# One-time chunk slots ahead of a weight ring, 32x32 block turns on the vector engine, and two w_down rows a partition in a one-core MoE encoder layer

## What is computed

```python
logits = xf @ w_router + b_router           # 32 experts
top_val, top_idx = lax.top_k(logits, 4)
gates = softmax(top_val)
# for each expert e, over the tokens that chose it:
hu = xb @ w_gate_up[e] + b_gate_up[e]       # 1024 -> 2 * 1024
a = minimum(hu[:, :1024], 7)
lin = clip(hu[:, 1024:], -7, 7)
act = a * sigmoid(1.702 * a) * (lin + 1)
y[tok] += (act @ w_down[e] + b_down[e]) * g
# then a last norm over x + y
```

## Time and profile before

| | us |
|---|---|
| median of 3 runs | 1447.47 |
| the profiled execution | 1449.7 |
| its span, from the first to the last instruction | 1447.7 |
| TensorE busy | 1354.7 |
| VectorE busy | 495.0 |
| ScalarE busy | 241.2 |
| GpSimd busy | 380.3 |

### The profile page before, as it was taken

How to read it: one execution, slowest core, us unless ns; L and a number is a source line. 1 busy time by engine, 2 the same in 40 slices (tenths; PEclk the granted TensorE clock), 3 DMA queues, 4 the chain that set the end, 5 groups by cost and what they waited for, 6 DMA issues and landing times.

```text
span 1447.7 us, 34000 instructions
## 1 busy us (share of the span) xinstructions
PE 1354.7 (94%) x14238; PEld 669.4 (46%) x14238; DVE 495.0 (34%) x791; ACT 241.2 (17%) x378; POOL 380.3 (26%) x298
## 2 busy tenths in 40 slices
PE   4899999987999999999999999999999999999982
PEld 4876777862444444444444433333344434344431
DVE  5555553552222223332322222222233333223222
ACT  4333333220111111111111111111111111111112
POOL 6834237034122211211122222111122111111110
PEclk9999999989999999999999999999999999999996
DMA  7511112565999999999999999999999999999994
GB/s 210 129 33 55 59 59 93 223 253 213 364 388 381 385 380 374 381 373 378 390 382 371 377 393 378 371 383 371 373 380 382 379 379 383 371 378 393 391 376 131
DMA packets 112780, 451.12 MB, mean 312 GB/s; under 512 B 14065, under 2 KB 38657, under 8 KB 79952
## 3 DMA queue, kind: packets, MB, share of 16 engines
q1 hardware_dynamic: 99664, 426.27, 77.1%
q0 software_dynamic: 10768, 19.86, 6.0%
q10 hardware_dynamic: 2320, 4.59, 0.8%
HBM read 440.01 MB, written 19.25 MB: 317 GB/s over the span
## 4 chain that ended last, share of the span: by engine, by line
DMA 62%; PE 27%; DVE 5%; issue 3%; ACT 2%; POOL 1%; SPq 1%; DVEq 0%; ACTq 0%; POOLq 0%
DMA raw<-in_w_gate_up_dram 16%; DMA raw_b<-in_w_down_dram 16%; DMA raw_a<-in_w_down_dram 15%; DMA raw_c<-in_w_gate_up_dram 14%; PE bank L1423 8%; PE bank L1439 4%; PE bank L1199 4%; PE bank L1201 4%; PE bank L1200 4%; DVE probs L977 1%; PE bank L1289 1%; ACT probs L720 1%; PE bank L1253 1%; DVE probs L964 1%; PE bank L1387 1%
## 5 line engine op out<-in xcount | busy, mean ns | idle before, releaser
L1423 PE MATMUL bank<-raw,xT 128*32 128x512 f32 x2304 | 343.7, 594 | 8.6 <-issue 4.1
L1425 PE MATMUL bank<-raw,xT 128*32 128x512 f32 x768 | 339.3, 594 | 0.2
L1125 DVE TENSOR_TENSOR gate_in<-bank,b_bc 96x512 f32<-96x512 f32 x64 | 41.1, 682 | 643.9 <-PE bank L1425 643.9
L1423 PEld LDWEIGHTS bank<-raw,xT 128*32 128x32 f32 x2304 | 90.6, 110 | 230.3 <-issue 189.5
L1439 PE MATMUL bank<-raw_a,aT 128*32 128x256 f32 x2232 | 166.8, 380 | 0.0
L1442 PE MATMUL bank<-raw_a,aT 128*32 128x256 f32 x744 | 166.4, 380 | 0.0
L1423 PE MATMUL bank<-raw_c,xT 128*32 128x512 f32 x1116 | 165.5, 592 | 0.0
L1425 PE MATMUL bank<-raw_c,xT 128*32 128x512 f32 x372 | 164.7, 592 | 0.0
L577 POOL DMA_INDIRECT sum_rows<-y_out,scatter_list x32 | 47.4, 1482 | 443.2 <-ACT y_out L831 364.6
L1439 PEld LDWEIGHTS bank<-raw_a,aT 128*32 128x32 f32 x2232 | 88.8, 110 | 62.1
L1439 PE MATMUL bank<-raw_b,aT 128*32 128x256 f32 x1152 | 93.1, 393 | 13.8 <-DMA raw_b<-in_w_down_dram 10.2
(11 more groups left out here) (227 smaller groups left out, 2259.1 us busy)
## 6 DMA issues: line engine op xcount, KB each, us to landing
raw<-in_w_gate_up_dram SPq DMA_DIRECT2D x128, 1024.0 KB
raw_c<-in_w_gate_up_dram SPq DMA_DIRECT2D x62, 1024.0 KB, 7.7
raw_a<-in_w_down_dram SPq DMA_DIRECT2D x62, 1024.0 KB
raw_b<-in_w_gate_up_dram SPq DMA_DIRECT2D x32, 1024.0 KB, 5.6
raw_b<-in_w_down_dram SPq DMA_DIRECT2D x32, 1024.0 KB, 9.1
raw_e<-in_w_gate_up_dram SPq DMA_DIRECT2D x31, 1024.0 KB
raw_d<-in_w_down_dram SPq DMA_DIRECT2D x31, 1024.0 KB
raw<-in_w_in_dram SPq DMA_DIRECT2D x24, 512.0 KB, 5.3
```

The source lines that it names most:

```text
L1125: dve.tensor_tensor(gate_in[0:TILE, cols], bank[n][0:TILE, :], b_bc[0:TILE, cols], ALU.add)
L1423: pe.matmul(bank[r][c * GROUP:(c + 1) * GROUP, :], xT[:, i, c * GROUP:(c + 1) * GROUP], w[:, r * 512:(r + 1) * 512], start=first, stop=last)
L1425: ins = pe.matmul(bank[r][TILE:P, :], xT[:, i, r * GROUP:(r + 1) * GROUP], w[:, 1536:2048], start=first, stop=last)
```

## The change

Four things. (1) Chunks 0 to 5 go to six slots of their own, used once; from chunk 6 on there is a ring of 12, so there are 18 slots, in memory that lay unused behind the front (`raw_f`, `raw_g`). Chunk m from 18 on still waits for chunk m - 12 to be used. (2) TensorE's 16 transposes a job and ScalarE's four copies are gone: VectorE turns `x_got` into `xT` (`turn_x`) and `lin_in` into `aT` (`turn_act`) by 12 transposes of 32x32 blocks each, straight in SBUF. (3) A down chunk puts rows 2p and 2p + 1 of `w_down` in partition p, one run of 8 KB in place of two of 4 KB; `turn_act` reads the activations with a stride of two to match. (4) The order of the jobs' parts: on VectorE `take_gu(j)`, `turn_x(j + 1)`, `clamp(j)`, `gate(j)`, `take_y(j - 1)`, `turn_act(j)`; GpSimd scatters job j - 1 (before: j - 2) in job j, loads the scatter list before it spreads the down biases, and spreads the gate-up biases ahead of the scatter; the loops start at job 2 on all engines but TensorE, where it starts at job 1.

```diff
-RAW = 12
+AHEAD, RING = 6, 12
+RAW = AHEAD + RING
...
-            for ring in (raw01, raw_a, raw_d, raw_b, raw_e, raw_c):
-                if m < ring.shape[1]:
-                    return ring[:, m, :]
-                m -= ring.shape[1]
+        def slot_of(m):
+            return m if m < AHEAD else AHEAD + (m - AHEAD) % RING
+        def raw_slot(slot):
+            for ring in (raw01, raw_a, raw_f, raw_d, raw_b, raw_g, raw_e, raw_c):
+                if slot < ring.shape[1]:
+                    return ring[:, slot, :]
+                slot -= ring.shape[1]
+        def loads(m, b):
+            return 16 if m < AHEAD else later(16 * ((m - AHEAD) // RING + 1), b, 16)
...
-                sp.dma_start(raw_slot(m % RAW).rearrange("p (i n) -> p i n", i=2),
-                             w_down[0, e, 2 * i * P:2 * (i + 1) * P, :].rearrange("(i p) n -> p i n", p=P))\
-                  .then_inc(w_loaded[m % RAW], 16)
...
+                sp.dma_start(raw_slot(slot_of(m)).rearrange("p (i n) -> p i n", i=2),
+                             w_down[0, e, 2 * i * P:2 * (i + 1) * P, :].rearrange("(p i) n -> p i n", i=2))\
+                  .then_inc(w_loaded[slot_of(m)], 16)
+            def wait_slot(m, b):
+                used = fixed(sp, later(m - (RING - 1), b, JOB)) if m >= RAW else 0
                 if m >= RAW:
                     sp.wait_ge(w_used, used)
                     return
...
                 elif m == RAW_FRONT + 2:
+                    sp.wait_ge(mT_hi_ready, KD)
+                    sp.wait_ge(mT_lo_ready, KD)
+                elif m == RAW_FRONT + 4:
                     sp.wait_ge(lists_emptied, 16)
-                elif m == RAW_FRONT + 3:
+                elif m == RAW_FRONT + 5:
                     wait_used(sp, N_FRONT - 1)
-                elif m == RAW_FRONT + 5:
+                elif m == RAW_FRONT + 11:
                     sp.wait_ge(ss_1_ready, TT)
-                elif m == RAW_FRONT + 6:
+                elif m == RAW_FRONT + 12:
                     sp.wait_ge(router_ready, TT)
...
                 gather(j + 1)
-                if n > 1:
-                    dn_loads = scatter(j - 2, lambda: fixed(pool, j * 16))
-                else:
-                    dn_loads = j * 16
-                gu_loads = fixed(pool, j * 16 + 16)
+                gu_loads = fixed(pool, j * 16 + 32)
+                pool.wait_ge(b_gu_loaded, gu_loads)
+                dn_loads = fixed(pool, j * 16 + 16)
+                spread_gu()
+                row = scatter(j - 1, lambda: list_row(j))
                 pool.wait_ge(b_dn_loaded, dn_loads)
-                pool.wait_ge(b_gu_loaded, gu_loads)
-                row = list_row(j - 1)
+                load_scatter_list(j, row)
                 spread_dn()
-                spread_gu()
-                load_scatter_list(j - 1, row)
+            pool.wait_ge(b_dn_loaded, 16)
+            spread_dn()
+            load_scatter_list(0, list_row(0))
+            pool.wait_ge(b_gu_loaded, 32)
+            spread_gu()
             job(1)
-            count = bodies(pool)
+            count = jobs_after(pool, 2)
             with pool.Fori(0, count) as b:
...
+                job(2, b)
...
-                load_bias_gu(j)
-                if n > 1:
-                    scale_y(j - 2)
-                    load_bias_dn(j - 1)
-                turned(j - 1, aT, act_turned, aT_ready)
-                turned(j + 1, xT, got_turned, xT_ready)
+                load_bias_gu(j + 1)
                 sigmoid(j)
-            turned(1, xT, got_turned, xT_ready)
+                scale_y(j - 1)
+                load_bias_dn(j)
+            take_picks()
+            load_bias_gu(1)
+            sigmoid(0)
             job(1)
...
+            def take_gu(j, used):
...
                 ins.then_inc(gu_taken, 1)
+            def turn_x(j):
+                dve.wait_ge(x_gathered, j * 16)
+                for g in range(GROUPS):
+                    rows = x_got[g * GROUP:(g + 1) * GROUP, :].rearrange("t (k q p) -> t k q p", q=QUADS, p=GROUP)
+                    for q in range(QUADS):
+                        ins = dve.transpose(xT[q * GROUP:(q + 1) * GROUP, :, g * GROUP:(g + 1) * GROUP], rows[:, :, q, :])
+                ins.then_inc(got_turned, 1)
...
+            def turn_act(j, used):
+                dve.wait_ge(act_ready, j + 1)
+                if not (isinstance(j, int) and j == 0):
+                    dve.wait_ge(w_used, used)
+                for g in range(GROUPS):
+                    rows = lin_in[g * GROUP:(g + 1) * GROUP, :].rearrange("t (i q p h) -> t i h q p", q=QUADS, p=GROUP, h=2)
+                    for q in range(QUADS):
+                        ins = dve.transpose(aT[q * GROUP:(q + 1) * GROUP, :, g * GROUP:(g + 1) * GROUP]
+                                            .rearrange("p (i h) t -> p i h t", h=2), rows[:, :, :, q, :])
+                ins.then_inc(aT_ready, 1)
...
                 j = job_no(dve, n, b)
-                if n > 1:
-                    take_y(j - 2, later(dn_chunk(n - 2, DN_CHUNKS - 1) + 1, b, BODY * JOB))
-                clamp(j, later(gu_chunk(n, GU_CHUNKS - 1) + 1, b, BODY * JOB))
+                gu_end, dn_end = gu_chunk(n, GU_CHUNKS), dn_chunk(n - 1, DN_CHUNKS)
+                take_gu(j, later(gu_end, b, JOB))
+                turn_x(j + 1)
+                clamp(j)
                 gate(j)
+                if n:
+                    take_y(j - 1, later(dn_end, b, JOB))
+                turn_act(j, later(dn_end, b, JOB))
+            job(0)
...
+                pe.wait_ge(got_turned, j)
                 for i in range(GU_CHUNKS):
                     m = gu_chunk(n, i)
-                    gate_up(m, i, turns[m // RAW])
-                    if i == 3:
-                        turn_act(j - 1)
-                pe.wait_ge(aT_ready, j * 2)
-                transpose_got(j + 1)
-                if n > 1:
-                    pe.wait_ge(y_taken, j - 1)
+                    gate_up(m, i, turns[(m - AHEAD) // RING - (gu_chunk(n, 0) - AHEAD) // RING])
+                pe.wait_ge(aT_ready, j)
                 for i in range(DN_CHUNKS):
```

More of the change, by code:

```diff
@@ L59 @@
 GROUPS = TILE // GROUP
+QUADS = P // GROUP
 QUARTER = D_MODEL // 4
@@ L296, in job_no, with loads_of @@
         def job_no(eng, n, b):
-            return fixed(eng, later(n, b, BODY))
-        def turns_of(eng, b):
-            return [fixed(eng, later(16 * (turn + 1), b, 16 * TURNS)) for turn in range(TURNS + 2)]
+            return fixed(eng, later(n, b, 1))
+        def loads_of(eng, first_m, b):
+            return {m: fixed(eng, loads(m, b)) for m in (first_m, AHEAD + ((first_m - AHEAD) // RING + 1) * RING)}
         def is_split(i):
@@ L322, in first_half, with jobs_after @@
             return ring[:, 0, :].rearrange("p (k two n) -> p k two n", k=KD, two=2)[:, :, n, :]
-        def bodies(eng):
+        def jobs_after(eng, first):
             eng.wait_ge(extra_ready, 1)
             extra = eng.value_load(extra_sb[0:1, 0:1], min_val=0, max_val=ROUNDS - 1)
-            jobs = extra * E + (E - FIRST + BODY - 1)
-            return eng.snap(jobs if BODY == 1 else (jobs * 171) >> 9)
+            return eng.snap(extra * E + (E - first))
         def wait_used(eng, s):
@@ L425, in _ @@
             sp.dma_start(g_fin_row[:, :], final_norm_g.partition_broadcast(P)).then_inc(g_fin_loaded, 16)
-            stored, used = (fixed(sp, later(FIRST * n, count, BODY * n)) for n in (16, JOB))
+            stored, used = (fixed(sp, later(2 * n, count, n)) for n in (16, JOB))
             sp.wait_ge(y_stored, stored)
@@ L1160, in take_y @@
                 ins.then_inc(y_taken, 1)
-            clamp(0, GU_CHUNKS)
-            gate(0)
             def job(n, b=0):
                 j = job_no(dve, n, b)
-                if n > 1:
-                    take_y(j - 2, later(dn_chunk(n - 2, DN_CHUNKS - 1) + 1, b, BODY * JOB))
-                clamp(j, later(gu_chunk(n, GU_CHUNKS - 1) + 1, b, BODY * JOB))
+                gu_end, dn_end = gu_chunk(n, GU_CHUNKS), dn_chunk(n - 1, DN_CHUNKS)
+                take_gu(j, later(gu_end, b, JOB))
+                turn_x(j + 1)
+                clamp(j)
                 gate(j)
+                if n:
+                    take_y(j - 1, later(dn_end, b, JOB))
+                turn_act(j, later(dn_end, b, JOB))
+            job(0)
             job(1)
-            count = bodies(dve)
+            count = jobs_after(dve, 2)
             with dve.Fori(0, count) as b:
-                for n in range(FIRST, FIRST + BODY):
-                    job(n, b)
-            end = fixed(dve, later(FIRST, count, BODY))
-            take_y(end - 2, later(FIRST * JOB - DN_CHUNKS, count, BODY * JOB))
-            take_y(end - 1, later(FIRST * JOB, count, BODY * JOB))
+                job(2, b)
+            take_y(fixed(dve, later(1, count, 1)), later(2 * JOB, count, JOB))
             dve.wait_ge(g_fin_loaded, 16)
@@ L1397, in _, with gate_up @@
                     ins.then_inc(places_1_ready, 1)
```

(25 more changed lines are left out.)

107 lines of the change are left out of this document (40 added, 67 removed).

## The result

The changed kernel takes 1618.7 us (median of 4 runs, 1617.0 to 1620.0) against 1447.9 us for the kernel before on the same chip: a ratio of 1.116, with a 95% interval from 1.114 to 1.118. Forecast were 1660 us, with a range from 1565 to 1710. The profiled execution has a span of 1618.1 us.

What follows compares the result with a forecast made beforehand. Transfers bound the kernel before at 34.4 us a job; a closed ring of waits would take over at 40.75. The start, 29 rounds (1181.75 us), the last round and the end gave 1660 us, range 1565 to 1710.

Steps and rivals of the forecast that it cites:

- What bounds the kernel: Loop of the kernel before: weight transfers set a beat of 34.4 us a job, TensorE 1.6 us a job behind.
- part 5: New order on VectorE and GpSimd: waits from one turn_x to the next close on themselves, 40.75 us a job.
- the ring: Chain turn_x, take_y, scatter, list loads, gather, turn_x, once a job without overlap: 40.75 us against the transfers' 34.4.
- The sum: Whole run: start, 29 rounds of 40.75 us, last round and end give a span of 1659.8 us, forecast 1660.
- Part 1: Transposes and copies taken off TensorE and ScalarE: TensorE's beat falls from 32.9 to 31.2 us, worth nothing by itself.
- Part 2: Six more slots: chunk 20 issued at 361.8, before at 361.25; gain 0, plus or minus 2 us.
- Part 3: Down chunks in runs of 8 KB: 4 us saved in the run, in so far as transfers stay the bound.
- Part 4: VectorE's turns: 0.42 us a transpose, 5.0 us for 12, hidden behind TensorE's down with 1.4 us to spare.
- Part 5's clock: TensorE idling 9 us a job lowers its granted clock: some 2 us a job of 11 us cover, nothing in time.
- B: Transfers stay the loop's bound, scatter, list and gather falling to 17 us in sum: 1445 us, 1438 to 1450; chance 0.10.
- C: VectorE's 4-byte block transposes take two passes, 0.84 us each, 10 us a turn: 1810 us; chance 0.06.
- D: Six slots and longer runs bring full worth, 17 and 4 us, nothing else moves: 1427 us; chance part of B's.

Runs made afterwards that it cites:

- the first experiment: The changed kernel with GpSimd's order alone altered, the gather of job j + 2 issued at the start of its job j, ahead of the scatter: 1453.6 us, ratio 1.003.
- run 41: Not a label, but part of "the run 41 us" longer: the kernel before with a loop body of three jobs, still 12 slots, 1489.2 us, ratio 1.028.

## Why the prediction was right, point by point

**What bounds the kernel, and part 5.** Right, and it decided the case. The steps of the ring, from the end of `turn_x`, with their start times in the fences above:

| step | forecast us | measured us |
|---|---|---|
| `clamp` and `gate` | 3.9 | 3.9 (795.20 to 799.13) |
| `take_y` | 2.35 | 2.35 (799.13 to 801.48) |
| `scale_y`, start of the scatter | 2.1 | 2.3 (to 803.79) |
| scatter to scatter list | 10.1 | 8.6 (to 812.38) |
| to the gather list | 2.7 | 1.8 (to 814.14) |
| to the gather | 6.6 | 5.9 (to 820.02) |
| the gather lands | 8.0 | 9.0 (to 829.03) |
| `turn_x` | 5.0 | 5.4 |
| round | 40.75 | 39.2 |

The mean of 29 rounds is 39.33 us (396.3 to 1536.75). I took the landings from the kernel before with full DMA engines; with these at 0.87 to 0.94 the scatter's landing is 7.7 instead of 9.0. Two latencies shrank a little, the loop's turn cost nothing, and the gather was longer than my guess between the bounds. That the 1.0 us of the gather stands against 3.1 of the three steps before it is luck: the guess for the gather rested on no row of its own. By the rule of the Trainium skill, "DMA: Bandwidth & Descriptors", section "Anatomy of one DMA", scatter and gather would have been 2.9 us each, as an estimate: they took 7.7 and 9.0, so the trace doesn't agree, and the rival that rested on it is gone.

**The sum.** Forecast 1659.8 of span, measured 1618.1, so 41.7 us too much. The start was 5.1 us later than forecast (`turn_x(2)` ends at 396.3, not 391.2), 3.4 of them at `take_gu(0)`. The 29 rounds of 39.33 instead of 40.75 are 41.2 us less. The last round took 31.8 instead of 36.75: `turn_x(32)` didn't wait at all and started at 1563.14 behind `take_gu(31)`, so the empty gather saved more than the half of 8.0 that I had taken off, and TensorE's work became the longer way. After it 0.5 us less: the last `down` took 12.5 us, not 13.4, the steps before it 0.6 more, and the end behind it 0.2 less. Together 5.1 - 41.2 - 5.0 - 0.5 = -41.6. That the late start and the short last round cancel is luck as well; the 1.4 us a round are the real miss.

**Part 1** is right: TensorE's part of a job fell, and nothing came of it. With the gather first, where TensorE sets the beat of the first rounds, they take 31.5 us (mean of seven) against 32.9. **Part 2** is right in kind: chunk 20 waited for the first chunk of `gate_up(1)` and was issued no earlier than before. But it was issued at 368.68, not at 361.8. `gate_up(1)` began 3.9 us later than forecast, and the granted clock was 0.50 from 363 to 367 us, after TensorE had stood still. Under the ring this cost nothing in the beat. What the sum felt is that "nothing before it changes" is wrong. The early chunks collide with a store in the front, and `take_gu(0)` came 3.4 us later. **Part 3** is right in kind; in the size it is half. I priced three chunks with down chunks among them as if all three were: 0.11 / 3 = 0.037 us a down chunk, and measured were 0.30 / 4 = 0.075 in the kernel before. **Part 4** took 0.42 us for a transpose, and it is 0.45 from start to start, 5.37 for twelve; the turn of 5.4 us lies within the cover, as the first experiment shows. **Part 5's clock** is right too: the slower start of `gate_up` costs 1.8 us a job of the cover, where 2 were forecast, and nothing in time. The DMA share was 0.88 from 400 to 1530 us, forecast 0.85.

**The rivals.** B, the transfers stay the bound, is refuted: scatter, list and gather took 7.7 + 5.9 + 9.0 = 22.6 us and not 17. It would have needed the rows some 5 us earlier in each round (39.3 against 34.4), and the row with 29 waits stands against it. C, two passes a transpose, is refuted by the 5.37 us. D needed B, and the kernels with 12 and 18 slots show that its six chunks bring nothing.

## What to carry to other kernels

When work moves to another engine or an order changes, follow each wait through the in-order queues until it comes back to where it began: a chain that closes on itself once a job sets the beat, whatever the busy shares are, and no step of it overlaps with another. Such a ring is best opened in the queue, by issuing the prefetch ahead of the wait for something slow: that gave back 165 us here, while a step made faster gives back only its own microseconds a job. It is tested by the same extra work in two places, one inside it and one outside.

## What the runs showed of the hardware that I had not expected

- VectorE's product of two tensors in SBUF (96x1024 floats) takes 1.22 to 1.28 us without and 3.06 us when a partition broadcast of GpSimd runs beside it. In the rows above the product starts at 925.14 and ends 0.9 us after the broadcast's end at 927.27. The transposes, with one input, are not touched: 438 ns beside the broadcast and 436 without it. By the Trainium skill, "SBUF — State Buffer", section "SBUF: two separate sides", an operation of VectorE with two SBUF inputs and one of GpSimd that reads SBUF exclude each other for the whole instruction. The rows agree for nearly all of it: alone the product takes 1.22 us, so 0.3 us of it fall before the broadcast's recorded end. The broadcast itself took 2.54 us there, but also 2.49 beside the transposes, and 2.29 in the changed kernel; in the first two it came right behind an indirect DMA of the same queue, so the product isn't shown to lengthen it.
- TensorE pays for a stop twice. It stood still for 4.6 to 5.7 us, and then its granted clock was 0.50 to 0.57 for some 4 us, at or near the level of 1.2 GHz. The mean granted clock was 0.92 in the changed kernel, which stops in every job.
- A loop body of three jobs instead of one made the job across each of the loop's ten turns 8 us longer, and the run 41 us.
- A store of 512 KB took 3.2 us beside little traffic and 10.0 us beside prefetched chunks (medians of four). A prefetch is not free when something small on the critical path crosses it.
